# Seven-product feed-forward in all four stages, with GpSimd making the weight sums of the last one

## The chip, the cores and the metric

One core of one Trainium2 chip. The metric is the device time of one execution in microseconds (us). A program like this keeps five engines going at once: TensorE (PE; its weight loads are listed as PEld), VectorE (DVE), ScalarE (ACT), GpSimd (POOL) and SyncE (SP), which issues the DMAs. Each runs its own instructions in order and waits for the others on semaphores.

## The reference

Two transformer blocks in fp32, one after the other, at 512 latent and 256 context tokens, D = 1024. The change lies in the second block, in its feed-forward half steps:

```python
def swiglu(x, w13, w2):
    a, b = jnp.split(x @ w13, 2, axis=-1)
    return (jax.nn.silu(a) * b) @ w2

def ffn_half_step(h, g, shift, scale, gate, w13, w2):
    return h + 0.5 * gate * swiglu(modulate(rms_norm_2(h, g), shift, scale), w13, w2)

for i in range(DEPTH):                      # DEPTH = 2
    h = ffn_half_step(h, ...ffn1[i])        # latents; hc likewise for the context
    ...mixing of latents and context...
    h = ffn_half_step(h, ...ffn2[i])
    if not last:
        hc = ffn_half_step(hc, ...ffn2[i])
```

`w13` is 1024 x 5632 and `w2` 2816 x 1024. The half step runs four times: three times on all T = 768 tokens, and the last time, where the context isn't wanted any more, on 512.

## The kernel before, in words

Activations lie feature-major: 8 row tiles of 128 features x C tokens, C = 768 or 512. An fp32 product is made from three products of rounded parts: every operand is split into a high part (a rounding copy by ScalarE: `w_hi`, `x_hi`, `g_hi`) and a low part (VectorE subtracts the high one: `w_lo`, `x_lo`, `g_lo`), and `triple` issues high x high, high x low and low x high. All matmuls of these stages are 128 x 128 weights against H = C/2 columns (384 or 256), or against a full segment of up to 512.

**Units and slots.** The 2816 hidden features are 22 tiles. A unit ("g", u, 0) makes hidden tile u: its two weight tiles (a and b of swiglu) come with one DMA of 1 MB into one of two landing buffers. A unit ("w", c, j) multiplies four hidden tiles into half of the output rows, from another 1 MB. After the g units 4, 8, 12 and 16 come the two w units of the four tiles before; at the end come w units 4 and 5 (the last one only two tiles). A unit is cut into parts, and a part is a slot: 12 matmuls, with one split weight quarter of 128 x 512 in a ring (`SH`, `SL`).

**Seven products.** Plain, a unit's 2 x 2 blocks want eight quarter products. The first two g units are plain (`plain_group`, all four quarters together). The others use Strassen's form (Winograd's variant) with seven (P1 to P7), each with sums of operands: sums of the normed input (`x_sum`: three per row tile pair, and `F4`), made once a stage; sums of the weights, four a unit, which overwrite the landing buffer (`b11 = b12 - b11`, `b12 = b22 - b12`, `b11 = b22 - b11`, `b21 = b21 - b11`); and for the second product sums of the hidden tiles (`g_sum`). Weight quarter P5 can be split only when sum 1 is made, P7 after sum 2, P6 after sum 3, P4 after sum 4. The parts P4 and P3 of a unit are held back and run between the first parts of the next (`held`).

**Two functions.** `ffn_sevens` (L1388) runs the three 768-token stages, and uses seven products for the first *and* the second matmul. Its ring holds 8 slots. VectorE makes the weight sums of g units, GpSimd those of w units. `ffn` (L909) runs the last stage, 512 tokens: seven products only for the first matmul; the second is plain (L1092, eight parts a chunk of four tiles, 12 matmuls of 512 columns each), and VectorE makes the weight sums (L1257). Its ring holds 11.

**Order of the work.** Nothing plans at run time: every engine walks the same list of slots. TensorE runs `quarter`, `second` and `last_two`; ScalarE and VectorE run `after(n)`, which waits for slot n and does what is due then: copies and silus, `gated`, `add_bank`, `add_out` (a product is added to the residual, twice a slot, L1845), `g_low` (L1822), `g_sum`, and at the end `split` for the slots whose ring places are free. In a w unit a bank collects several products one after the other, and VectorE must have added the sum so far before the next product goes onto it (`out_done`). `first_done` tells that the first half of a slot is there, `slot_done` that all is.

**The opening of a stage.** ScalarE and VectorE make the normed input tile by tile, while `plain_group(0)` follows them. Then come the input sums: x_sum, ScalarE's high copy, VectorE's low part, four times in turn, and only then does either engine go on to `after(0)`, with the gates of the plain groups and the splits of slot 8 and later. `plain_group(1)` runs meanwhile.

Of the kernel before, what the change touches and what calls it, by code (L numbers as in the profile page):

```python
# [22 lines left out]
P = 128  # L23
# [367 lines left out]
class Kernel:  # L391
# [517 lines left out]
    def ffn(self, layer, which, segs, m, gain, tag, following):  # L909
# [7 lines left out]
        parts = [(c, c0, n, o, n // 2) for (c, (c0, n)), o in zip(enumerate(segs), (0, LAT // 2))]  # L917
        shift, scale, gate = m(0), m(1), m(2)
        PLAIN, RING, GR = 2, 11, 6
        A11, A21, A12, A22, S1, S2, S4 = range(7)  # L920
        S3 = A21
        P1, P2, P5, P7, P6, P4, P3 = range(7)
        operand_of = (A11, A12, S1, S3, S2, A22, S4)
        bank_of = (0, 1, 2, 0, 0, 0, 2)

        units = []
        for u in range(FT):
            units.append(("g", u))
            if u % 4 == 0 and 4 <= u <= 16:
                units.append(("w", u // 4 - 1))  # L930
        units += [("w", 4), ("w", 5)]
        slots, loads, begin = [], [], {}
        for kind, u in units:
            begin[kind, u] = len(slots)
            if kind == "g":
                loads.append((kind, u, 0))
                slots += [(kind, u, part, len(loads) - 1) for part in range(4 if u < PLAIN else 7)]
            else:
                for j in range(2 if u < 5 else 1):
                    loads.append((kind, u, j))  # L940
                    slots += [(kind, u, 4 * j + part, len(loads) - 1) for part in range(4)]
        Q = len(slots)
        last_slot = [max(q for q in range(Q) if slots[q][3] == n) for n in range(len(loads))]
        tiles_of = lambda c: range(4 * c, min(4 * c + 4, FT))
        order, held = [], []
        for kind, u in units:
            q = begin[kind, u]
            if kind == "g" and u < PLAIN:
                order += [q, q + 1, q + 2, q + 3]
            elif kind == "g":  # L950
                order += [q + P1] + held + [q + P2, q + P6, q + P5, q + P7]
                held = [q + P4, q + P3]
            else:
                order += [q] + held + list(range(q + 1, q + (8 if u < 5 else 4)))
                held = []
        assert sorted(order) == list(range(Q))
        place_of = {q: n for n, q in enumerate(order)}
        used_up = lambda q: place_of[last_slot[slots[q][3]] if slots[q][0] == "g" and slots[q][1] < PLAIN else q] + 1
        ended = lambda kind, u, part: place_of[begin[kind, u] + part] + 1
        splits_at, nxt = [], RING  # L960
        for n in range(Q):
            splits_at.append([])
            if nxt < Q and used_up(nxt - RING) <= n + 1:
                splits_at[-1].append(nxt)
                nxt += 1
            assert n + 1 == Q or order[n + 1] < nxt
        outs_before = lambda c: 8 * c

        AHt, ALt, GHt, GLt, SHt, SLt, temps, early = self.place(tag, [
            ("x_hi", 7 * 4 * 384, F32R), ("x_lo", 7 * 4 * 384, F32R), ("g_hi", GR * T, F32R), ("g_lo", GR * T, F32R),  # L970
            ("w_hi", RING * 512, F32R), ("w_lo", RING * 512, F32R), ("ffn_tiles", 3 * 384 + 2 * T, F32),
            ("x_full", 2 * GR * T, F32, 2 * 7 * 4 * 384)])
        AH, AL = (t[:, 0:28 * H].rearrange("p (o k n) -> p o k n", o=7, k=4) for t in (AHt, ALt))
        GH, GL = (t.rearrange("p (s n) -> p s n", n=T)[:, :, 0:C] for t in (GHt, GLt))
        SH, SL = (t.rearrange("p (s k n) -> p s k n", k=4, n=P) for t in (SHt, SLt))
        land = self.land
        X1, X2, X3 = (temps[:, H * n:H * n + H] for n in range(3))
        X123 = temps[:, 0:3 * H].rearrange("p (o n) -> p o n", o=3)
        SG = [temps[:, 1152 + T * n:1152 + T * n + C] for n in range(2)]
        full_at = (2, 3, 4, 5, 8, 9, 10, 11)  # L980
        F = [early[:, T * a:T * a + C] for a in full_at]
        F4 = early[:, 2 * T:6 * T].rearrange("p (k n) -> p k n", n=T)
        halves = lambda t: t.rearrange("p (h n) -> p h n", h=2)
        pair_of = lambda t, k: t[:, 2 * (k // 4):2 * (k // 4) + 2, k % 4]
        A = self.small[:, 48:64].rearrange("p (k c) -> p k c", c=2)
        half = self.small[:, 32:48].rearrange("p (k c) -> p k c", c=2)
        tt, stt, mm = nc.vector.tensor_tensor, nc.vector.scalar_tensor_tensor, nc.tensor.matmul
        bank = lambda b, n=H: PS[:, b * 512:b * 512 + n]
        spans = [(0, C)] if C <= 512 else [(0, H), (H, H)]
# [10 lines left out]
        for kind, u in units:  # L1000
            if kind == "w":
                at_bank += at_bank % 2
# [16 lines left out]
        with nc.Block() as block:  # L1019
            @block.sync  # L1020
            def _(sp):
# [7 lines left out]
                if following:  # L1029
                    sp.wait_ge(wlo.h, wlo.at(0, Q))  # L1030
# [3373 lines left out]
```

## Time and profile before

| | us |
|---|---|
| median of 3 runs (lowest, highest) | 4178.95 (4173.89, 4184.53) |
| the profiled execution: its own time | 4179.97 |
| its span | 4178.2 |
| TensorE busy | 3951.5 |
| VectorE busy | 2753.9 |
| ScalarE busy | 1827.6 |
| GpSimd busy | 373.9 |
| mean granted TensorE clock | 0.978 |

Busy is the time in which an instruction of the engine ran. Matmuls are pipelined, so that their records overlap: one of 384 columns is listed with 334 ns, though the next starts 173 ns after it. The start-to-start distance is the price. In the lists, "[0.42 <-DVE g_lo L1822]" is idle time before an instruction and who ended it.

### The profile page before, as it was taken

Reading aid. Unit: us, or ns where it says so; the run is one execution under the profiler, and the core shown is the slowest. Engines: PE = TensorE matmul, PEld = TensorE weight load, DVE = VectorE, ACT = ScalarE, POOL = GpSimd, SP = SyncE. Lnnn points to the kernel's source line nnn. Section 1 sums busy time; section 2 is a strip of 40 time slices with the busy share of each in tenths; the row PEclk is TensorE's granted clock in tenths of the full one; section 3 lists DMA queues with packets and bytes.
Section 4 is the critical chain, followed back from the end, with each engine's and each line's share of the span. In section 5 each row is a group of like instructions: output and inputs, shape, how many; then the busy total and the mean of one; then the engine's idle time right before and its main releaser. Section 6 shows DMA issues by size and latency. Waiting matters only on the chain. (4 is left out here: it accounts for less than half of the span.)

```text
span 4178.2 us, 93191 instructions
## 1 busy us (share of the span) xinstructions
PE 3951.5 (95%) x40440; PEld 3512.1 (84%) x40440; DVE 2753.9 (66%) x4362; ACT 1827.6 (44%) x3172; POOL 373.9 (9%) x279
## 2 busy tenths in 40 slices
PE   6999999998999998999999989999999999989999
PEld 5778877777788887899997768999989999668998
DVE  6555665555444443788885457888878887657776
ACT  4433433342255554544443425444454444445443
POOL 0111111011000000011111020111111111120000
PEclk9999999999999998999999999999999999999999
DMA  4001010003345455112121101221212212112222
GB/s 173 19 14 28 27 28 28 17 14 136 146 167 182 176 178 222 51 71 72 71 71 75 59 31 51 71 71 71 73 49 71 71 71 81 65 58 78 103 103 81
DMA packets 99880, 337.05 MB, mean 81 GB/s; under 512 B 5009, under 2 KB 66834, under 8 KB 71826
## 3 DMA queue, kind: packets, MB, share of 16 engines
q1 hardware_dynamic: 99474, 331.09, 22.2%
q8 instruction: 321, 5.26, 0.5%
q14 instruction: 85, 0.70, 0.1%
HBM read 326.62 MB, written 4.46 MB: 79 GB/s over the span
## 5 line engine op out<-in xcount | busy, mean ns | idle before, releaser
L1547 PE MATMUL banks<-x_hi,w_hi 128*128 128x384 f32 (+2 forms) x1968 | 662.7, 337 | 21.5 <-ACT banks L1708 7.9
L1548 PE MATMUL banks<-x_lo,w_hi 128*128 128x384 f32 (+2 forms) x1968 | 660.0, 335 | 0.0
L1549 PE MATMUL banks<-x_hi,w_lo 128*128 128x384 f32 (+2 forms) x1968 | 659.7, 335 | 0.0
L1670 ACT CAST w_hi<-landing_all 128x512 fp32r<-128x512 f32 x666 | 406.9, 619 | 463.0 <-PE banks L1549 172.9
L1787 DVE TENSOR_TENSOR w_lo<-landing_all,w_hi 128x512 fp32r<-128x512 f32 x666 | 478.8, 739 | 60.0 <-ACT w_hi L1670 58.8
L1547 PEld LDWEIGHTS banks<-x_hi,w_hi 128*128 128x128 f32 x1968 | 371.1, 189 | 31.0 <-ACT banks L1708 8.8
L1548 PEld LDWEIGHTS banks<-x_lo,w_hi 128*128 128x128 f32 x1968 | 371.2, 189 | 2.0
L1549 PEld LDWEIGHTS banks<-x_hi,w_lo 128*128 128x128 f32 x1968 | 371.1, 189 | 2.0
L1547 PE MATMUL banks<-g_hi,w_hi 128*128 128x384 f32 x840 | 283.6, 338 | 12.9 <-DVE x_res L1845 7.8
L1549 PE MATMUL banks<-g_hi,w_lo 128*128 128x384 f32 x840 | 280.9, 334 | 0.0
L1548 PE MATMUL banks<-g_lo,w_hi 128*128 128x384 f32 x840 | 280.9, 334 | 0.0
L1845 DVE SCALAR_TENSOR_TENSOR x_res<-banks,small,x_res 128x384 f32<-128x384 f32 x540 | 228.8, 473 | 12.1 <-PE banks L1549 12.1
L2193 PE MATMUL banks<-rw_x_hi_rwkv,rw_w_hi_rwkv 128*128 128x256 f32 (+1 forms) x512 | 190.7, 372 | 7.9 <-ACT small L2597 4.5
L1646 POOL TENSOR_TENSOR landing_all<-landing_all 128x512 f32<-128x512 f32 x30 | 38.8, 1293 | 1759.8 <-DVE w_lo L1787 1759.8
L1045 PE MATMUL banks<-x_hi,w_hi 128*128 128x256 f32 x624 | 179.2, 287 | 5.5 <-ACT ffn_tiles L1175 2.0
L1047 PE MATMUL banks<-x_hi,w_lo 128*128 128x256 f32 x624 | 177.2, 284 | 0.0
L2194 PE MATMUL banks<-rw_x_lo_rwkv,rw_w_hi_rwkv 128*128 128x256 f32 (+1 forms) x512 | 177.2, 346 | 0.0
L1046 PE MATMUL banks<-x_lo,w_hi 128*128 128x256 f32 x624 | 177.2, 284 | 0.0
L2195 PE MATMUL banks<-rw_x_hi_rwkv,rw_w_lo_rwkv 128*128 128x256 f32 (+1 forms) x512 | 176.7, 345 | 0.0
L1547 PEld LDWEIGHTS banks<-g_hi,w_hi 128*128 128x128 f32 x840 | 157.6, 188 | 22.3 <-issue 12.7
L1548 PEld LDWEIGHTS banks<-g_lo,w_hi 128*128 128x128 f32 x840 | 157.7, 188 | 0.0
L1549 PEld LDWEIGHTS banks<-g_hi,w_lo 128*128 128x128 f32 x840 | 157.7, 188 | 0.0
(548 smaller groups left out, 9283.5 us busy)
## 6 DMA issues: line engine op xcount, KB each, us to landing
landing_all<-in_w SPq DMA_DIRECT2D x132, 1024.0 KB, 4.8
arena_first<-in_ada_w SPq DMA_DIRECT2D x38, 2048.0 KB, 8.6
weight_ring_first<-in_rw_pair SPq DMA_DIRECT2D x32, 512.0 KB, 5.0
landing_all<-in_w_in SPq DMA_DIRECT2D x12, 1024.0 KB, 4.8
weight_ring_first<-in_da_head SPq DMA_DIRECT2D x16, 512.0 KB, 9.8
weight_ring_first<-in_da_head SPq DMA_DIRECT2D x8, 1024.0 KB, 6.2
landing_all<-in_w_out SPq DMA_DIRECT2D x8, 1024.0 KB, 4.8
x_normed_first<-in_ada_w SPq DMA_DIRECT2D x3, 2048.0 KB, 10.7
```

The costliest lines, as they stand in the source:

```text
L1045: mm(o, wh, xh, start=first, stop=False, skip_group_check=onto)
L1046: mm(o, wh, xl, start=False, stop=False, skip_group_check=onto)
L1047: return mm(o, wl, xh, start=False, stop=last, skip_group_check=onto)
L1547: mm(o, wh, xh, start=first, stop=False, skip_group_check=onto)
L1548: mm(o, wh, xl, start=False, stop=False, skip_group_check=onto)
L1549: return mm(o, wl, xh, start=False, stop=last, skip_group_check=onto)
L1670: nc.scalar.copy(SH[:, q % RING], raw(q)).then_inc(whi.h, 1)
L1787: tt(SL[:, q % RING], raw(q), SH[:, q % RING].bitcast(F32), ALU.subtract).then_inc(wlo.h, 1)
L1845: ins = stt(xs, PS[:, at + c0:at + c0 + cn], half[:, x, c:c + 1], xs, ALU.mult, ALU.add)
L2193: mm(o, wh, xh, start=kt == 0, stop=False)
L2194: mm(o, wh, xl, start=False, stop=False)
L2195: ins = mm(o, wl, xh, start=False, stop=kt == KT - 1)
```

## The change

1. `ffn` is gone, and `ffn_sevens` takes its name and a parameter `segs`; sizes follow C = 768 or 512. The last stage, at 512 tokens (H = 256), so gets seven products in the second matmul too, and the ring of 8.
2. Weight sums of g units are VectorE's only for C = 768; in the 512-token stage GpSimd makes them, as it does those of the w units.
3. The order of slots: a w unit that follows a g unit holds P3 of that unit back to behind P6, and P3 comes behind P7. In the last unit the held part comes behind the first.
4. `second` issues the two halves' first inner tile (k = 0) before it waits for the hidden tiles (`glo`), then k = 1 of both halves; so `first_done` comes after 9 of 12 matmuls instead of 6.
5. The input sums get two buffers, and are interleaved with `after(0)` to `after(4)`.
6. The banks of the last eight outputs are taken in the order in which they come free.

```diff
-    def ffn(self, layer, which, segs, m, gain, tag, following):
...
-    def ffn_sevens(self, layer, which, m, gain, tag, following):
+    def ffn(self, layer, which, segs, m, gain, tag, following):
...
+        by_vector = lambda unit: unit[0] == "g" and C == T
...
             if unit not in sevens:
-                slots += held + [(unit, part) for part in range(4)]
+                slots += [(unit, 0)] + held + [(unit, 1), (unit, 2), (unit, 3)]
...
             else:
-                slots += [(unit, P1)] + held[0:1] + [(unit, P2)] + held[1:2] + [(unit, P5), (unit, P6), (unit, P3), (unit, P7)]
+                slots += [(unit, P1)] + held[0:1] + [(unit, P2), (unit, P5), (unit, P6)] + held[1:2] + [(unit, P7), (unit, P3)] if held[1:2] else \
+                    [(unit, P1)] + held + [(unit, P2), (unit, P5), (unit, P6), (unit, P3), (unit, P7)]
...
-        first_sums = temps[:, 2 * H + 2 * T:5 * H + 2 * T].rearrange("p (o n) -> p o n", o=3)
+        first_sums = [temps[:, a:a + 3 * H].rearrange("p (o n) -> p o n", o=3) for a in (2 * H + C, 5 * H + C)]
...
     def second(q):
-                    pe.wait_ge(glo.h, glo.at(0, 4 * unit[1] + (3 if part in (P1, P2, P4) else 4)))
                     pe.wait_ge(wlo.h, wlo.at(0, q + 1))
+                    at = [bank_at(unit, part, ab) for ab in range(2)]
                     for ab in range(2):
...
-                        for k in range(2):
-                            ins = triple(bank(b), SH[:, r, 2 * ab + k], SL[:, r, 2 * ab + k], OH[:, x, k], OL[:, x, k], k == 0 and first, k == 1, not first)
+                        triple(bank(at[ab]), SH[:, r, 2 * ab], SL[:, r, 2 * ab], OH[:, x, 0], OL[:, x, 0], first, False, not first)
+                    pe.wait_ge(glo.h, glo.at(0, 4 * unit[1] + (3 if part in (P1, P2, P4) else 4)))
+                    for ab in range(2):
+                        ins = triple(bank(at[ab]), SH[:, r, 2 * ab + 1], SL[:, r, 2 * ab + 1], OH[:, x, 1], OL[:, x, 1], False, True, not first)
                         ins.then_inc((first_done if ab == 0 else slot_done).h, 1)
...
             @block.gpsimd
                 for unit, s in sevens.items():
-                    if unit[0] == "g":
+                    if by_vector(unit):
                         continue
...
                 def gate_half(u, h, src):
-                    elif u >= PLAIN:
+                    elif u >= 1:
                         act.wait_ge(sums_lo.h, sums_lo.at(0, 4))
...
             @block.scalar
-                for at in range(4):
-                    x_sums(at)
-                for n in range(Q):
+                x_sums(0)
+                after(0)
+                after(1)
+                x_sums(1)
+                after(2)
+                after(3)
+                x_sums(2)
+                x_sums(3)
+                for n in range(4, Q):
                     after(n)
...
             @block.vector
-                for at in range(4):
-                    x_sum(at)
-                    if at == 3:
-                        L.mark(tt(F4[:, :, 0:H], F4[:, :, 0:H], F4[:, :, H:T], ALU.subtract), sums_made)
-                    x_sum_low(at)
-                for n in range(Q):
+                x_sum(0)
+                x_sum(1)
+                x_sum_low(0)
+                for n in range(4):
+                    after(n)
+                x_sum(2)
+                x_sum_low(1)
+                after(4)
+                x_sum(3)
+                x_sum_low(2)
+                L.mark(tt(F4[:, :, 0:H], F4[:, :, 0:H], F4[:, :, H:C], ALU.subtract), sums_made)
+                x_sum_low(3)
+                for n in range(5, Q):
                     after(n)
```

## Rows read from the trace of the kernel before

**Rows 1.** The page, part 1: busy us (share) xinstructions by engine
```profile
PE 3951.5 (95%) x40440; PEld 3512.1 (84%) x40440; DVE 2753.9 (66%) x4362; ACT 1827.6 (44%) x3172; POOL 373.9 (9%) x279
```

**Rows 2.** Windows (stretch, length, busy by engine, PEclk, DMA): two stages, two chunks
```profile
1708.00:2215.00 507.00, 496.07 (x2814) 487.75 (x2814) 420.86 (x694) 236.57 (x414) 62.23 (x43) 0.99 0.19 69
3805.00:4170.00 365.00, 357.74 (x2442) 331.99 (x2441) 283.20 (x488) 177.02 (x354) 6.43 (x5) 0.99 0.25 90
1885.70:1974.50 88.80, 87.95 (x505) 87.28 (x505) 74.80 (x125) 40.27 (x74) 11.14 (x8) 1.00 0.20 72
3921.90:3984.40 62.50, 62.50 (x433) 58.39 (x433) 48.99 (x85) 29.32 (x60) 0.00 (x0) 1.00 0.28 102
```

**Rows 3.** Timeline of TensorE (start, duration): first and last of three unbroken runs
```profile
1829.67 0.33 PE L1548 MATMUL banks<-x_lo,w_hi 128*128 128x384 f32 x1
...
1833.84 0.33 PE L1548 MATMUL banks<-x_lo,w_hi 128*128 128x384 f32 x1
...
3899.73 0.28 PE L1045 MATMUL banks<-x_hi,w_hi 128*128 128x256 f32 x1
...
3911.13 0.28 PE L1047 MATMUL banks<-x_hi,w_lo 128*128 128x256 f32 x1
...
4151.64 0.39 PE L1045 MATMUL banks<-g_hi,w_hi 128*128 128x512 f32 x1
...
4162.29 0.39 PE L1047 MATMUL banks<-g_hi,w_lo 128*128 128x512 f32 x1
```

**Rows 4.** Waits of TensorE, 1706 to 3570 us: total, times, longest
```profile
PE banks L1547 <- ACT banks L1708: 7.9, 3, 2.6
PE banks L1547 <- DVE x_res L1845: 7.8, 15, 1.0
PE banks L1547 <- ACT ffn_tiles L1708: 7.4, 3, 3.5
PE banks L1547 <- DVE g_lo L1822: 5.1, 12, 0.4
...
PE banks L1547 <- DVE w_lo L1787: 3.5, 3, 1.2
```

**Rows 5.** TensorE around one such wait, and the window behind an opening's waits
```profile
1884.97 0.34 PE L1549 MATMUL banks<-x_hi,w_lo 128*128 128x384 f32 x1
1885.73 0.44 PE L1547 MATMUL banks<-g_hi,w_hi 128*128 128x384 f32 x1 [0.42 <-DVE g_lo L1822]
1886.01 0.34 PE L1548 MATMUL banks<-g_lo,w_hi 128*128 128x384 f32 x1
...
3101.00:3121.00 20.00, 17.54 (x90) 17.22 (x91) 18.90 (x28) 10.94 (x21) 0.00 (x0) 0.91 0.15 53
```

**Rows 6.** Timeline of VectorE in the opening of the third stage
```profile
3074.75 0.55 DVE L1854 TENSOR_TENSOR ffn_tiles<-x_full 128x384 f32<-128x384 f32 x1
...
3077.71 1.36 DVE L1861 TENSOR_TENSOR x_lo<-ffn_tiles,x_hi 128x1152 fp32r<-128x1152 f32 x1 [1.23 <-ACT x_hi L1702]
```

**Rows 7.** Timeline: VectorE beside GpSimd's weight sums, 1874 to 1894 us
```profile
1874.51 3.38 DVE L1787 TENSOR_TENSOR w_lo<-landing_all,w_hi 128x512 fp32r<-128x512 f32 x2 [0.24 <-ACT w_hi L1670]
1880.64 1.28 DVE L1787 TENSOR_TENSOR w_lo<-landing_all,w_hi 128x512 fp32r<-128x512 f32 x2
...
1892.82 1.13 DVE L1845 SCALAR_TENSOR_TENSOR x_res<-banks,small,x_res 128x384 f32<-128x384 f32 x2
...
1874.36 1.29 POOL L1646 TENSOR_TENSOR landing_all<-landing_all 128x512 f32<-128x512 f32 x1 [60.96 <-DVE w_lo L1787]
1875.73 1.62 POOL L1648 TENSOR_TENSOR landing_all<-landing_all 128x512 f32<-128x512 f32 x1
```

**Rows 8.** Groups of VectorE: one chunk of the last stage, then adds in 768-token stages
```profile
L1249 DVE TENSOR_TENSOR w_lo<-landing_all,w_hi 128x512 fp32r<-128x512 f32 x36 | 24.1, 684 | 0.4 <-ACT w_hi L1152 0.4
L1257 DVE TENSOR_TENSOR landing_all<-landing_all 128x512 f32<-128x512 f32 x17 | 11.8, 692 | 0.6
...
L1260 DVE TENSOR_TENSOR ffn_tiles<-banks,ffn_tiles 128x256 f32<-128x256 f32 x12 | 5.1, 422 | 5.5 <-PE banks L1047 3.7 <-ACT ffn_tiles L1175 1.8
...
L1845 DVE SCALAR_TENSOR_TENSOR x_res<-banks,small,x_res 128x256 f32<-128x256 f32 x120 | 56.6, 472 | 0.0
```

More of the change, by code:

```diff
@@ L916, in ffn @@
         H, rstd_at = C // 2, 6 * 512
[L917 to L960, printed above, removed]
-        for n in range(Q):
[L962 to L989, printed above, removed]
-        sig = self.sig
-        gain_ready, half_ready, own = sig("norm_gain_ready"), sig("half_gate_ready"), sig("dve_order")
@@ L1414, in ffn_sevens @@
         loads = {unit: n for n, unit in enumerate(units)}
-        sevens = {unit: unit[1] - PLAIN if unit[0] == "g" else 2 * unit[1] + unit[2] for unit in units if (unit[1] >= PLAIN if unit[0] == "g" else unit[1] < 5)}
+        by_vector = lambda unit: unit[0] == "g" and C == T
+        in_sevens = [unit for unit in units if (unit[1] >= PLAIN if unit[0] == "g" else unit[1] < 5)]
+        sevens = {unit: sum(by_vector(x) == by_vector(unit) for x in in_sevens[:n]) for n, unit in enumerate(in_sevens)}
         slots, held = [], []
@@ L1788, in split @@
                     unit, part = slots[q]
-                    if unit[0] == "w" or unit not in sevens or part not in (P1, P5, P2):
+                    if unit not in sevens or not by_vector(unit) or part not in (P1, P5, P2):
                         return
@@ L1877, in after @@
                         for x in (2 * part, 2 * part + 1)[0:1 if part == 3 else 2]:
-                            residual(x, *parts[0])
-                            residual(x, *parts[1]).then_inc(out_done.h, 1)
+                            for at in tile_parts(x):
+                                ins = residual(x, *at)
+                            ins.then_inc(out_done.h, 1)
                         if part == 3:
@@ L1956, in ffn_sevens @@
         self.advance(1, last_done)
-        self.advance(4 * (FT - PLAIN), wsum)
-        self.advance(40, wsum2)
+        self.advance(4 * sum(map(by_vector, in_sevens)), wsum)
+        self.advance(4 * sum(not by_vector(unit) for unit in in_sevens), wsum2)
         self.advance(2 * (FT - PLAIN), u_made)
```

458 lines of the change are left out of this document (47 added, 411 removed).

## The prediction, made before the changed kernel ran

> **What bounds the kernel now.** First the page, part 1: TensorE is busy in 95% of the span, VectorE in 66%, GpSimd hardly [rows 1]. Then the windows, since that is a mean over stages. In a 768-token feed-forward stage TensorE works 496 of 507 us, in the 512-token one 358 of 365; VectorE is at 83% in a 768-token chunk (74.8 of 88.8 us) and at 78% in a 512-token chunk (49.0 of 62.5) [rows 2]. So these stages run at TensorE's rate, apart from its waits. Third, TensorE's timeline, for the price of a matmul, which is its start-to-start distance: 4.17 us over 24 steps is 0.174 us at 384 columns, 11.40 over 95 is 0.120 at 256, and 10.65 over 47 is 0.227 at 512 [rows 3]. 256 columns cost more than half of 512. Fourth, its waits: in the three 768-token stages 12.9 us of idle in 27 waits of w units (15 for `x_res`, 12 for `g_lo`), and 18.8 us in nine waits of the openings, three each [rows 4]. A wait costs more than its listed idle: behind the matmul of 1884.97 the next one is due at 1885.14 and starts at 1885.73, 0.59 us late for 0.42 listed, and its successor is 0.11 late again [rows 5]. I add 0.26 us to each. Behind an opening's waits the clock row shows 0.91 over 20 us: 3.6 us at the 1.2 GHz level instead of 2.4, which costs 1.8 us of matmuls [rows 5].
>
> **Chunk order and the split in `second` (768 tokens).** At most 12.9 + 27 x 0.26 = 19.9 us come off. The `g_lo` wait is 0.6 us long, and now half a slot, 6 x 0.174 = 1.04 us, is issued ahead of it: gone. The `x_res` waits stand where P4 follows P7 of the unit before with one slot between; now there are two. The last five of them are longer (up to 1.0 us) and lie before the last unit, where a whole slot is put in between. Against it: `first_done` comes after nine matmuls, 0.52 us later, and TensorE wants the second half's bank 0.52 us sooner. VectorE's two adds take 1.1 us [rows 7] of a 2.08 us slot, so I expect room for it. The deferred P3 also frees its landing buffer two slots later, three slots or 6.2 us before the next load's first split; at 512 tokens that is 4.3 us, but the ring of 8 lies between. Bounds: 10 us (the `x_res` waits stay) to 20. I take **-18.5**.
>
> **Openings (768 tokens).** They cost 18.8 + 9 x 0.26 + 3 x 1.8 = 26.5 us. Today VectorE waits 1.23 us for ScalarE in three of the four input sums [rows 6], and neither splits slot 8 before all four are made. With two buffers the three waits go, 3.7 us an opening, and the first weights of unit 2 are early, so the `w_lo` wait (3.5 us in all) goes. What is late next: VectorE has the same work as before up to unit 3 and is behind, so it, or ScalarE, whose gates of unit 1 now wait for all four low parts, makes TensorE wait again, for the copy of P1 (about 1 us) and at P4 of unit 2 (2 to 3 us). So some 4.2 us an opening are won, of at most 8.8: **-12.5**, bounds 0 and -26.
>
> **Last stage, TensorE.** Out: 5 chunks x 96 matmuls x 0.227 = 109.0 us. In: 5 x 168 x 0.120 = 100.8. **-8** if TensorE stays the bound.
>
> **Last stage, VectorE.** A chunk becomes 42 slots of 1.44 us = 60.5 us of TensorE. VectorE's list for it: 42 splits at 0.684 (28.7), 24 adds to the residual at 0.472 (11.3), 16 sums with products and gates at 0.422 (6.8) [rows 8], and for the hidden tiles two low parts of 256 and two of 512 elements, eight sums at 0.42 and two low parts of 1024 at some 1.2: 8.0. That is 54.8 us of durations in 96 instructions. Back to back they overlap (two splits in 1.28 us, not 1.37 [rows 7]), and some wait a little for a semaphore: 48.5 us, about the 49.0 of today. Gone are 16 sums at 0.69 and eight adds at 0.75; new are six splits, 24 adds and the hidden sums. So GpSimd does not empty VectorE, it keeps it level.
>
> And GpSimd's sums, 24 a chunk, are not free for VectorE. Two splits take 1.28 us alone and 3.38 us beside sums L1646 and L1648: 1.05 us lost for a sum. Two adds that read PSUM take 1.13 us beside L1646 and lose nothing [rows 7]. So a sum costs between 0 and 1.05 us by what it meets. In g units nearly everything of VectorE's is splits and other work on SBUF: I take 0.8 for 16 sums. In w units half is adds from PSUM: 0.5 for eight. Together 16.8 us, and 48.5 + 16.8 = 65.3 > 60.5: VectorE becomes the bound. Today's chunk is 62.5, so five chunks are +14. The opening keeps its waits: unit 2's P5 and P6 now wait for GpSimd's sums of 1.29 us instead of VectorE's 0.69: +1.5. **+15.5** for the stage, bounds -9 (65.3 falls to 60.7 when the sums cost 0.5 or less each) and +40 (1.05 each in g units, 0.6 in w units: 70.1).
>
> The Trainium skill ("SBUF — State Buffer", section "Who interferes with whom") says that a VectorE instruction with two SBUF inputs and a GpSimd one that reads SBUF exclude each other for the whole instruction, whoever comes first. The trace agrees on which instructions suffer, and less on how much: a full block would make the two splits 4.0 us, and they took 3.4. By the rule the sum is that of the rival "full block".
>
> **Sum.** -18.5 - 12.5 + 15.5 = -15.5. The profiled execution took 1.8 us beyond its span of 4178.2, so 4180.0, and the median is 1.0 below: 4179 - 15.5 = 4163.5, say 4164.
>
> **Rivals.**
> *GpSimd's sums cost VectorE little* (0.5 us or less): VectorE ends a chunk in 60.5, TensorE stays the bound. For it: VectorE idles 13.5 us a chunk today, into which lost time could fall, and a third of its new work reads PSUM. Against: the splits come just when a sum is released by one. 4179 - 31 - 9 + 1.5 = 4140.
>
> *Full block*: each sum stops VectorE's SBUF work for all of its length. Sums last 1.29 to 1.62 us [rows 7]; with three quarters of them met by such work, 24 x 1.45 x 0.75 = 26 us, a chunk 74.6, +60.5 for five, in all 4179 - 31 + 62 = 4210; at 1.05 and 0.6 as above it is 4188. It decides when a sum costs over 0.84 us on average (chunk above 68.7, which eats the 31 us). For it: the 3.38 us. Against: the adds that lose nothing.
>
> *Only the place of the waits moves (768 tokens)*: VectorE at 83% is behind in openings and w units alike; the later `first_done` makes it late for P7 and P3, whose banks wait for its adds. Then 12 us come off instead of 31: 4179 - 12 + 15.5 = 4182. For it: every wait of the w units but the twelve is on VectorE's adds. Against: the distances between products of one bank grow where the waits are.
>
> **Chances.** Mine 0.47 (own range 4150 to 4178), cheap sums 0.18, full block 0.15, waits that move 0.20. From 4137 to 4192 leaves out the far end of the cheap sums and most of the full block. A difference of 0.3%, 12.5 us, is what a measurement of this kernel can tell: below 4166.5 lie six tenths of mine and nearly all of the cheap sums, 0.48 with a little of the third; above 4191.5 most of the full block and a little of the third, 0.16; between them 0.36.
>
> **What would show it.** Right: in a chunk of the last stage VectorE busy over 95% in a period of 64 to 67 us, TensorE waiting for `w_lo` or `x_res`; splits beside GpSimd's sums at 1.0 us and more; in the 768-token stages no TensorE wait for `g_lo`, hardly one for `x_res`, period 87.5; openings with one wait of 1 and one of 2 to 3 us. Wrong: a period of 60.5 (cheap sums), over 69 (full block), new waits at P7 or P3 in w units, or openings without any wait, which would be worth 14 us more than I give.

## The result and the profile after

Measured: 4244.69 us median of four runs (4237.47 to 4250.43) against 4178.95 before, a ratio of 1.016 with a 95% interval of 1.0145 to 1.0175. The change makes the kernel slower; the forecast was 4164, its range ended at 4192. It was wrong.

The page, part 1, of the kernel after (busy us, share, instructions) answers to [rows 1]:
```profile
PE 3964.6 (93%) x40800; PEld 3538.6 (83%) x40800; DVE 2827.1 (67%) x4422; ACT 1848.5 (44%) x3232; POOL 539.9 (13%) x399
```
VectorE (DVE) is 73 us busier, GpSimd (POOL) 166. A share of the span says nothing of where that hurts, so next the windows of the same stretches as [rows 2], and a chunk of a 768-token stage (stretch, length, busy by engine, PEclk, DMA):
```profile
1708.00:2215.00 507.00, 495.14 (x2832) 487.84 (x2830) 417.19 (x689) 233.76 (x412) 65.85 (x45) 1.00 0.19 69
3805.00:4170.00 365.00, 306.97 (x2367) 298.78 (x2366) 304.07 (x458) 172.20 (x349) 151.87 (x108) 0.96 0.23 81
...
1874.90:1963.90 89.00, 87.99 (x504) 87.26 (x504) 74.59 (x125) 39.69 (x73) 11.09 (x9) 1.00 0.20 72
```
The 768-token stage looks as before. In the 512-token one TensorE works 307 of 365 us instead of 358, while no other engine is full: VectorE is at 83%.

From TensorE's timeline I take each stage's length, from its first product matmul to its last. The rows for the last stage, after:
```profile
3806.06 0.47 PE L1076 MATMUL banks<-x_hi,w_hi 128*128 128x256 f32 x1
...
4233.85 0.28 PE L1078 MATMUL banks<-x_hi,w_lo 128*128 128x256 f32 x1
```
That is 427.8 us. Before it was 354.3, read the same way. The three 768-token stages were 503.7, 505.3 and 503.5 us before (1512.5 in sum) and are 503.0, 505.4 and 506.3 after (1514.7). So the last stage takes 73.5 us more and the long stages gained nothing; the rest of the spans' difference of 69.0 us (4247.2 less 4178.2) lies ahead of the first of them, which starts 6.5 us earlier in this execution, in code that the change doesn't touch.

One chunk of the last stage has two parts: the **g part**, 25 slots of gate units, and the **w part**, from the first product of its w units to the last. Windows of the second chunk, before and after:
```profile
3892.54:3930.39 37.85, 37.85 (x313) 37.53 (x312) 32.80 (x58) 21.72 (x46) 0.00 (x0) 1.00 0.31 112
3930.39:3955.08 24.69, 24.69 (x123) 20.91 (x121) 16.23 (x26) 7.60 (x14) 0.00 (x0) 1.00 0.24 86
```
```profile
3906.50:3951.92 45.42, 39.47 (x302) 38.86 (x301) 34.91 (x47) 21.91 (x48) 22.30 (x16) 0.92 0.20 71
3951.92:3982.89 30.97, 25.87 (x207) 24.80 (x205) 28.46 (x51) 12.76 (x26) 11.55 (x9) 1.00 0.29 103
```
The first pair is before: 62.5 us, TensorE always busy, VectorE at 87% and 66%. The second is after: 76.4 us, VectorE busy for 63.4 of them, but at 77% in the g part and 92% in the w part. The 42 slots of 1.44 us would be 36.0 and 24.5 us (25 and 17 slots; three of the 17 belong to gate units: the held P4 and P3, and P1 of the next one). So the g part is 9.4 us late, the w part 6.5.

Who waits, in the last stage after (waiter, releaser: us in total, times, longest):
```profile
ACT w_hi L1201 <- POOL landing_all L1182: 99.8, 29, 5.8
...
PE banks L1076 <- ACT ffn_tiles L1239: 40.7, 16, 5.1
ACT w_hi L1201 <- POOL landing_all L1177: 40.0, 26, 3.8
...
ACT w_hi L1201 <- DMA landing_all<-in_w: 38.0, 21, 3.3
...
PE banks L1076 <- DVE x_res L1382: 19.5, 22, 2.3
```
ScalarE (ACT), busy for 47% of the window of this stage shown above, stands still for 99.8 us ahead of splits (L1201) whose input is GpSimd's third sum (L1182). What queues behind it is seen at one place, on ScalarE, GpSimd and TensorE (start, duration, engine, line, output<-input, idle before and its releaser):
```profile
3867.76 0.62 ACT L1201 CAST w_hi<-landing_all 128x512 fp32r<-128x512 f32 x1 [0.53 <-POOL landing_all L1177]
3873.09 0.62 ACT L1201 CAST w_hi<-landing_all 128x512 fp32r<-128x512 f32 x1 [4.70 <-POOL landing_all L1182]
3873.61 0.37 ACT L1239 COPY ffn_tiles<-banks 128x256 f32<-128x256 f32 x1
...
3867.81 1.63 POOL L1179 TENSOR_TENSOR landing_all<-landing_all 128x512 f32<-128x512 f32 x1
3871.79 1.26 POOL L1182 TENSOR_TENSOR landing_all<-landing_all 128x512 f32<-128x512 f32 x1 [2.36 <-DVE w_lo L1324]
...
3870.08 0.28 PE L1078 MATMUL banks<-x_hi,w_lo 128*128 128x256 f32 x1
3874.03 0.58 PE L1076 MATMUL banks<-x_hi,w_hi 128*128 128x256 f32 x1 [3.68 <-ACT ffn_tiles L1239]
3874.41 0.41 PE L1077 MATMUL banks<-x_lo,w_hi 128*128 128x256 f32 x1
3874.63 0.41 PE L1078 MATMUL banks<-x_hi,w_lo 128*128 128x256 f32 x1
```
The window from there on, with the clock at the end of the row:
```profile
3874.00:3877.00 3.00, 2.97 (x14) 2.97 (x15) 2.55 (x4) 2.11 (x6) 0.46 (x1) 0.50 0.01 3
```
TensorE had ended P6 and waited for its copy (L1239) before P7. The copy stood in ScalarE's order behind the split of a P6 that is needed many slots later, which waited for GpSimd, which waited for VectorE's split of P5. TensorE is 3.8 us late for it, and its next matmuls come every 0.22 us instead of 0.12, at a granted clock of 0.50: the lower clock level (1.2 GHz), a second price of the wait. The clock of the g part of the second chunk above is 0.92, before it was 1.00.

The same happened, smaller, in the 768-token stages. After (TensorE, then ScalarE):
```profile
1874.92 0.44 PE L1076 MATMUL banks<-x_hi,w_hi 128*128 128x384 f32 x1 [0.55 <-ACT ffn_tiles L1239]
...
1904.84 0.41 PE L1076 MATMUL banks<-g_hi,w_hi 128*128 128x384 f32 x1 [0.50 <-DVE x_res L1382]
...
1873.87 0.62 ACT L1201 CAST w_hi<-landing_all 128x512 fp32r<-128x512 f32 x1 [5.03 <-POOL landing_all L1182]
1874.40 0.47 ACT L1239 COPY ffn_tiles<-banks 128x384 f32<-128x384 f32 x1
```
The `g_lo` wait of [rows 5] is gone. In its place a wait of 0.72 us for the copy stands before a gate unit's P7, and 0.67 us for `x_res` are left. From 1874.92 to the same place of the next chunk it is 89.05 us; before it was 88.74, forecast was 87.5.

### The profile page after: what moved, and what is told of

It reads as the page before. It is cut to its first block and busy times, and to the rows that moved or that the text cites. A ratio compares the mean times of both kernels' runs of the same rounds, so it can differ in the third digit from the quotient of the medians.

```text
span 4247.2 us, 94269 instructions
## 1 busy us (share of the span) xinstructions
PE 3964.6 (93%) x40800; PEld 3538.6 (83%) x40800; DVE 2827.1 (67%) x4422; ACT 1848.5 (44%) x3232; POOL 539.9 (13%) x399
## 5 line engine op out<-in xcount | busy, mean ns | idle before, releaser
L1076 PE MATMUL banks<-x_hi,w_hi 128*128 128x384 f32 (+1 forms) x2610 | 857.8, 329 | 72.7 <-ACT ffn_tiles L1239 63.9
L1077 PE MATMUL banks<-x_lo,w_hi 128*128 128x384 f32 (+1 forms) x2610 | 850.5, 326 | 0.0
L1078 PE MATMUL banks<-x_hi,w_lo 128*128 128x384 f32 (+1 forms) x2610 | 850.5, 326 | 0.0
L1201 ACT CAST w_hi<-landing_all 128x512 fp32r<-128x512 f32 x888 | 537.9, 619 | 695.9 <-POOL landing_all L1182 250.5
L1324 DVE TENSOR_TENSOR w_lo<-landing_all,w_hi 128x512 fp32r<-128x512 f32 x888 | 669.5, 772 | 128.8 <-ACT w_hi L1201 124.8
L1077 PEld LDWEIGHTS banks<-x_lo,w_hi 128*128 128x128 f32 x2610 | 501.7, 192 | 2.7
L1078 PEld LDWEIGHTS banks<-x_hi,w_lo 128*128 128x128 f32 x2610 | 501.2, 192 | 2.6
L1076 PE MATMUL banks<-g_hi,w_hi 128*128 128x384 f32 (+1 forms) x1120 | 364.5, 325 | 26.3 <-DVE x_res L1382 25.7
L1077 PE MATMUL banks<-g_lo,w_hi 128*128 128x384 f32 (+1 forms) x1120 | 360.6, 322 | 0.0
L1078 PE MATMUL banks<-g_hi,w_lo 128*128 128x384 f32 (+1 forms) x1120 | 360.4, 322 | 0.0
L1382 DVE SCALAR_TENSOR_TENSOR x_res<-banks,small,x_res 128x256 f32<-128x256 f32 (+2 forms) x660 | 278.6, 474 | 6.5 <-PE banks L1078 6.3
```

Of the source, the lines that this page charges most:

```text
L1076: mm(o, wh, xh, start=first, stop=False, skip_group_check=onto)
L1077: mm(o, wh, xl, start=False, stop=False, skip_group_check=onto)
L1078: return mm(o, wl, xh, start=False, stop=last, skip_group_check=onto)
L1201: nc.scalar.copy(SH[:, q % RING], raw(q)).then_inc(whi.h, 1)
L1324: tt(SL[:, q % RING], raw(q), SH[:, q % RING].bitcast(F32), ALU.subtract).then_inc(wlo.h, 1)
L1382: ins = stt(xs, PS[:, at + c0:at + c0 + cn], half[:, x, c:c + 1], xs, ALU.mult, ALU.add)
```

## The experiments

The theories are called A (GpSimd's results come late, and ScalarE's fixed order passes that on), B (VectorE's time beside GpSimd), C (seven products cost it in themselves). The table gives the time of the last stage's products, and of the g and w part of its second chunk with VectorE's busy time in brackets, all us, read as above. But for x14 and x15 each run is a single execution. In the eight traces with the last stage of before its length is 354.3 to 354.4 us; the long stages, and what lies ahead of them, move by a few us from one execution to the next, so I compare stages and not whole times. No kernel with the new last stage was traced twice.

| run | stage | g part | w part |
|---|---|---|---|
| before | 354.3 | 37.9 (32.8) | 24.7 (16.2) |
| after | 427.8 | 45.4 (34.9) | 31.0 (28.5) |
| x1 gate units' sums on VectorE | 417.1 | 43.6 (35.5) | 30.3 (29.0) |
| x2 all sums on VectorE | 409.9 | 40.9 (34.7) | 32.1 (29.8) |
| x3 sums of 16 columns | 359.4 | 37.1 (25.2) | 26.3 (24.4) |
| x4 the same, idle sums beside | 404.8 | 42.5 (34.1) | 29.4 (27.0) |
| x5 third landing buffer, ring 12 | 412.5 | 38.3 (32.7) | 34.2 (30.9) |
| x6 later split of P6 | 423.3 | 43.6 (34.9) | 31.6 (29.9) |
| x9 x5, splits spaced | 409.7 | 38.3 (33.6) | 33.7 (30.9) |
| x13 thinned adds | 414.9 | 46.1 (35.5) | 27.6 (24.7) |
| x16 x9 and thinned adds | 402.9 | 39.7 (32.0) | 30.2 (26.6) |
| x17 third landing buffer | 414.6 | 44.8 (32.5) | 29.8 (28.4) |
| x18 ring 12 | 448.4 | 45.9 (33.8) | 33.3 (30.1) |

**x1 and x2: who makes the sums.**
```diff
-        by_vector = lambda unit: unit[0] == "g" and C == T
+        by_vector = lambda unit: unit[0] == "g"              # x1
+        by_vector = lambda unit: unit[0] == "g" or C < T     # x2
```


> Changed from the kernel after, in the 512-token stage alone: VectorE makes the four weight sums of each of the 20 gate units again (80 sums); the 40 of the w units stay with GpSimd. Theory A (what costs is that ScalarE, in its fixed order, waits for GpSimd's sums, and copies and gates queue behind it): two thirds of those waits go; VectorE gets 16 sums of 0.69 us in a chunk and loses the overlap with as many of GpSimd's (16 x 0.62), so its own time stays near 64 us; chunk 65 to 68 us instead of 76.4, the stage's products 365 to 380 us instead of 427.8. Theory B (VectorE's time beside GpSimd, the forecast's own step): its load is unchanged within 1 us, chunk 75 to 77, stage 420 to 430. Theory C (seven products cost it in themselves at 512 tokens): no change either, 425 to 430.

> As the kernel after, but in the 512-token stage VectorE makes all 120 weight sums and GpSimd none. VectorE's list is 48.5 + 24 x 0.69 = 65.1 us a chunk without any overlap with GpSimd. Theory A and theory B both: chunk 65 to 67, VectorE over 95% busy, stage 362 to 378 us. Theory C: chunk over 72, stage over 405 us, with VectorE under 90% busy.


Measured 4236.0 and 4236.2 us (before beside them 4176.5). Stages 417.1 and 409.9: 11 and 18 us less than after, not the 50 to 65 that A and B both wanted of x2. Without any GpSimd VectorE is busy for 64.5 us of a 73.0 us chunk, 93% in the w part and 85% in the g part: theory C's case as it was put. Over x3 below, the sums cost the stage 50.5 us on VectorE and 68.4 on GpSimd. And ScalarE's stand isn't GpSimd's alone: with the sums on VectorE it waits for the third one 29 times, as in the kernel after. From x2's waits, 3842 to 4210 us:
```profile
ACT w_hi L1201 <- DVE landing_all L1337: 86.3, 29, 5.1
```

**x3 and x4: nearly no sums, and idle ones that nobody waits for.**
```diff
-                    b11, b12, b21, b22 = quarters(unit)
+                    b11, b12, b21, b22 = [b if C == T else b[:, :, 0:4] for b in quarters(unit)]
+                    # x4 alone: full subtractions between spare tiles, as many as sums, each behind its pair or single sum
```


> As the kernel after, but in the 512-token stage GpSimd's 120 weight sums cover 16 of their 512 columns each; the rest of the sums is left out. Neither their latency nor their time beside VectorE is left. Theories A and B: TensorE is the bound at about 60.5 us a chunk, stage 340 to 352 us, time 4155 to 4170. Theory C: chunk over 70, stage over 395.

> As the kernel with the 16-column sums, but after each pair or single one GpSimd runs a full subtraction of 512 columns between spare tiles that nobody reads: its 120 long operations beside VectorE are back, without anyone waiting for their results. Theory A (latency in ScalarE's order): as the 16-column kernel within 10 us, 345 to 360 us for the stage. Theory B (VectorE beside GpSimd): VectorE loses its 0.6 us per operation again and the stage is 405 to 430 us. Theory C: no difference between the two, both over 395 us.


Measured 4174.6 and 4213.4 us. With nearly free sums the stage is 359.4: so 68 of the 73.5 us hang on the 120 sums. Of these the idle operations bring back 45.4, though nobody waits for their results, so theory B has a real part. How large it is against A's, x4 can't say: its splits take 0.82 us in the mean and those of the kernel after 0.89, so the remaining 23.0 hold some of B's price too; and the short sums stand behind the idle operations in GpSimd's order, so the 45.4 hold some waiting. Of the 5.1 us left over 354.3 no run shows the cause; the short sums are still a chain, and ScalarE still stands 47.3 us for the third ones. 359.4 lies in none of the ranges expected, nearest to A's and B's (352 at most); theory C, which wanted over 395, falls. Even with nearly free sums the seven products don't give the 8 us that TensorE's matmuls save.

VectorE's groups in the last stage of the kernel after, and in x2, where GpSimd is idle (busy us, mean ns):
```profile
L1324 DVE TENSOR_TENSOR w_lo<-landing_all,w_hi 128x512 fp32r<-128x512 f32 x196 | 171.4, 894 | 43.9 <-ACT w_hi L1201 41.2
L1382 DVE SCALAR_TENSOR_TENSOR x_res<-banks,small,x_res 128x256 f32<-128x256 f32 x96 | 41.6, 472 | 0.0
L1348 DVE TENSOR_TENSOR ffn_tiles<-ffn_tiles 128x256 f32<-128x256 f32 x38 | 30.8, 849 | 0.7
```
```profile
L1324 DVE TENSOR_TENSOR w_lo<-landing_all,w_hi 128x512 fp32r<-128x512 f32 x194 | 129.3, 686 | 25.7 <-ACT w_hi L1201 24.7
L1382 DVE SCALAR_TENSOR_TENSOR x_res<-banks,small,x_res 128x256 f32<-128x256 f32 x96 | 41.8, 478 | 0.1
```
A split is 0.21 us longer in the mean in the kernel after, an add that reads PSUM not at all. 196 x 0.21 is 41 us; a gate (L1348) takes 0.85 instead of some 0.42, 38 x 0.43 = 16 us. With some 10 more in the hidden tiles' sums and low parts that is 67 us for 111 sums, 0.6 us each; forecast was 0.7. The Trainium skill ("SBUF — State Buffer", section "Who interferes with whom") says that a VectorE instruction with at most one SBUF input, outside its two-port modes, doesn't contend with GpSimd and one with two does; the trace agrees on both.

The mean of 0.21 us hides three cases. In the timelines of the two engines, 3842 to 4200 us, 128 of the 196 splits meet no sum and take 0.69 us. Sixty begin while a sum runs and take 1.35; eight begin ahead of one and take 0.68, and then it is the sum that is longer. One that begins under a sum, VectorE's row first:
```profile
3885.31 0.99 DVE L1324 TENSOR_TENSOR w_lo<-landing_all,w_hi 128x512 fp32r<-128x512 f32 x1
...
3884.13 1.62 POOL L1179 TENSOR_TENSOR landing_all<-landing_all 128x512 f32<-128x512 f32 x1
```
It ends 0.55 us behind the sum. Of the 42 that meet one sum only 37 do so too, within 0.01 us, and the other five end 0.66 us behind it. That is a full block: the split does its work when the sum has ended. The same page of the Trainium skill states it (section "SBUF: two separate sides") for the whole instruction, for a VectorE instruction with two SBUF inputs and whoever starts first; the trace agrees. A sum costs 0.6 us and not its 1.3 to 1.7 because it isn't always met: of the sums' 155 us in this window VectorE's instructions with two SBUF inputs lie beside 97, and in some of these it is the sum that waits.

**x5, x9, x17 and x18: more room between the engines.** The 512-token tiles leave room for a third landing buffer and four more slots of the ring.
```diff
-        PLAIN, RING, RAW = 2, 8, 4
+        PLAIN, RING, RAW = 2, 8 if C == T else 12, 4     # x5, x9, x18
+        NL = 2 if C == T else 3                          # landing buffers; x5, x9, x17
...
+        # x9: splits of P5 and P6 at least two slots behind the split that their sum needs
```


> As the kernel after, but the 512-token stage has a third landing buffer and a ring of 12 split weights instead of 8 (room that its smaller tiles leave free); GpSimd makes the sums as before. Theory A' (the forecast's load was right, and what it missed is that the load comes in bursts: 28.5 us of VectorE's work in the 31 us of a chunk's w part, which a ring of 8 and two landing buffers don't carry over to the g part): with more room the burst is spread over the chunk and the period falls from 76.4 towards VectorE's own 63.8 us: 66 to 70 us, stage 372 to 392 us, VectorE 92% busy or more. Rival (the waits are round trips within a unit: TensorE's product, the copy or sum of it, TensorE's next product, none of which a ring shortens): chunk 74 to 77, stage 415 to 430 us.

> As the kernel with three landing buffers and a ring of 12 in the 512-token stage, and there the splits that need GpSimd's first and third sum stand at least two slots behind the one before them in their chain, so that ScalarE doesn't stand still ahead of its copies while GpSimd works. Theory E (ScalarE's in-order stand for the chain of sums makes the waits, and depth alone only moves it forward): period falls from 72.4 to 65 to 69 us, stage 378 to 395 us instead of 412.5. Theory F (VectorE's own lateness in the w part, and its slower instructions beside GpSimd, make them): no more than 5 us from 412.5.

> As the kernel after with a third landing buffer in the 512-token stage, the ring still 8. If the g part waits because a buffer comes free late (two units' sums and the load of 4.8 us in one cycle of two buffers), it falls from 46.3 to 38 to 40 us and the chunk to 70 to 72. If ScalarE's stand for GpSimd's third sum makes it, at most 3 us go.

> As the kernel after with a ring of 12 split weights in the 512-token stage and two landing buffers. If the landing buffer's cycle makes the g part's waits, the ring gives less than 3 us a chunk (74 to 77); if the lead of 8 slots is too short for ScalarE's stands, it gives what both together gave: 71 to 73.


Measured 4225.1, 4225.1, 4227.5 and 4262.5 us (before beside them 4171.9, 4176.7, 4171.9 and 4171.9). Windows of x9, second chunk:
```profile
3905.54:3943.82 38.28, 36.36 (x303) 36.10 (x302) 33.56 (x47) 21.67 (x47) 18.95 (x14) 1.00 0.27 99
3943.82:3977.52 33.70, 27.12 (x207) 26.20 (x206) 30.88 (x51) 13.41 (x27) 15.47 (x11) 0.95 0.23 76
```
Buffers and ring together free the g part (38.3 us, 2.3 over its products) and lengthen the w part, where VectorE is busy for 30.9 us: some of its load has moved there. The period falls to 72 us and no further (x5's 412.5 us lie between the two ranges expected); the spacing gives 2.8 us of the stage and not 17 or more, so theory E of x9 falls. The landing buffer alone gives 13 us of the stage, less than expected in the g part. The ring alone, forecast harmless, costs 21 us. ScalarE's waits in x18's last stage, 3798 to 4247 us:
```profile
ACT w_hi L1206 <- POOL landing_all L1187: 75.1, 29, 5.7
ACT w_hi L1206 <- DMA landing_all<-in_w: 73.1, 21, 4.9
```
It stands less for the third sums than in the kernel after (99.8), 11 us more for the first, and 35 us more for weights that have not landed (38.0): the first split of a unit now comes earlier in its order, ahead of the landing, and copies stand behind it. TensorE waits 56 us for copies instead of 43. With a third landing buffer the same ring costs nothing: 412.5 us in x5 against 414.6 in x17. So a deeper ring behind an in-order engine is not just more slack; here the buffers that feed it had to grow with it.

**x13 and x16: VectorE's burst in the w part.**
```diff
-                    for c, c0, cn in in_half[h]:
+                    for c, c0, cn in in_half[h] if C == T else [(c, c0, 16) for c, c0, _ in in_half[h]]:
```


> As the kernel after, but in the 512-token stage the second product's adds into the residual cover 16 columns instead of 256; the rest of these adds is left out. That takes some 7 to 9 us of VectorE's time out of a chunk's w part and leaves GpSimd's sums, their latency and the queues as they are. Theory F (VectorE's burst in the w part makes the stage long): w part from 31 to 24 to 27 us, chunk from 76.4 to 66 to 70, stage 370 to 395 us. Theory E (the latency of the sums in ScalarE's order): the stage stays within 10 us of 427.8.

> The kernel with three landing buffers, a ring of 12 and the spaced splits in the 512-token stage, and there the adds into the residual thinned to 16 columns (the rest of them is left out). If the two causes add up: g part 37 to 38.3 us, w part 24 to 28 us (from 33.4), chunk 62 to 66 us against 71.6 and 73.9 with one of them alone. If VectorE's burst alone or the buffers alone were the cause and the rest a fixed chain, the chunk stays at 70 or more.


Measured 4234.3 and 4221.7 us (before beside them 4174.2 and 4171.9). A thinned add takes 0.222 us instead of 0.472, 6 us for 24 of them and not 7 to 9. The w part fell from 31.0 to 27.6, the g part stayed. The stage is 12.9 us shorter, between the two theories' numbers: F is right about the w part and says nothing of the g part. Together with the deeper buffers the period is 69.9, not the 62 to 66 of two causes that add up. So neither is the whole of it.

**x6 and x7: the split of P6 behind the copy.**
```diff
-            while nxt < Q and used_up(nxt - RING) <= n + 1 and len(splits_at[n]) < 2:
+            late = slots[nxt][0] in sevens and not by_vector(slots[nxt][0]) and slots[nxt][1] == P6
+            while nxt < Q and used_up(nxt - RING) <= n + 1 - late and len(splits_at[n]) < 2:
```
(`late` is worked out anew for each `nxt`.) x7 has the last stage as before.


> As the kernel after, but where GpSimd makes the sums the split of the sixth product's weights stands one slot later in ScalarE's and VectorE's order, behind ScalarE's copy of the g unit's sixth product. In the 768-token stages TensorE's wait of 0.72 us for that copy in each chunk and the one of 2.16 us near the end should go: each stage 3 to 5 us shorter (products 499 to 502 instead of 503.0 to 506.3). In the 512-token stage the theory of latency in ScalarE's order has up to 23 us to give (the difference between the full sums and the 16-column sums with the idle operations beside them): 405 to 422 us instead of 427.8; if VectorE's own lateness makes the waits, it stays within 5 us of 427.8.

> The 512-token stage as in the kernel before (plain second product, ring of 11, no sums by GpSimd); the 768-token stages as in the kernel after, with the later split of the sixth product. The last stage returns to 354 us of products. If the later split removes the waits for the copy, the three long stages give 3 to 5 us each and the whole is 10 to 15 us under the kernel before: 4162 to 4170 on this scale (before 4179). If the waits only move once more: 4176 to 4181.


Measured 4226.8 and 4161.5 us (before 4171.9 beside both). The three long stages take 500.4, 501.8, 499.9 and 500.0, 503.2, 501.7 us, 1502.1 and 1504.9 in sum. The kernel after's code for them ran in eleven profiled executions of this study, with sums of 1510.7 to 1516.6: it is some 11 us shorter, more than that spread, and the wait for the copy inside the chunks is gone. x7's last stage is back at 354.4. In x6's last stage only 4.5 us of the 23 between x4 and the kernel after came.

**x8 and x12: one edit of the 768-token stages undone,** the last stage as before.
```diff
+                slots += [(unit, P1)] + held[0:1] + [(unit, P2)] + held[1:2] + [(unit, P5), (unit, P6), (unit, P3), (unit, P7)]  # x8
...
+                for at in range(4):        # x12, on VectorE; on ScalarE all four x_sums(at), then every slot
+                    x_sum(at)
...
+                    x_sum_low(at)
+                for n in range(Q):
+                    after(n)
```


> The 512-token stage as in the kernel before; the 768-token stages as in the kernel after, but with the kernel before's order of the w units' products. If the new order is what puts the split of the sixth product ahead of the copy, then TensorE's 0.72 us for the copy in each chunk is gone and the waits of 0.56 to 0.59 us for x_res are back at their old places; no wait for g_lo, since the second product's halves stand apart. Stages 500 to 503 us. If the new order is worth what was forecast for it, stages 506 to 510 us.

> The 512-token stage as in the kernel before; the 768-token stages as in the kernel after, but with the kernel before's opening: all four first sums made and split before anything of the first two units is served. The forecast gave the new opening 12.5 us over three stages (4.2 each); read from the two traces, the waits of the opening were 6.4 us before and 4.3 after, and the slow clock behind the long one is in both: the new one should be worth 1.5 to 2.5 us a stage, so here 504.5 to 508.5 us of products.


Measured 4156.3 (before 4171.9) and 4192.1 (before 4176.7). Sums of the long stages: 1507.8 with the old order, so the new order costs 7 us of them instead of giving any; 1523.7 with the old opening (508.9, 509.3, 505.5), so the new opening gives 9 us, 3 a stage, more than the 1.5 to 2.5 expected. x12 also gives order and halves together: in these stages it differs from the kernel before by them and little else (the banks of the last outputs), and is 11.2 us longer. In x8 the wait for the copy is gone from the chunks and two waits for `x_res` stand there instead of one: TensorE's waits, 1694 to 3542 us,
```profile
PE banks L1555 <- DVE x_res L1861: 12.9, 27, 1.0
PE banks L1555 <- ACT ffn_tiles L1718: 10.6, 3, 3.5
```
and its chunk is 88.85 us. The `g_lo` wait is gone there too, so the halves in `second` alone remove it, and a chunk is no shorter for it than the 88.74 before.

**x10 and x11: the later split at the opening too,** the last stage as before. In the opening ScalarE stood 2.85 us for VectorE's third sum of unit 3 ahead of the copy of unit 2's P6, and TensorE 3.70 us for that copy:
```profile
1754.52 0.69 PE L1076 MATMUL banks<-x_hi,w_hi 128*128 128x384 f32 x1 [3.53 <-ACT ffn_tiles L1239]
```
```diff
+            late = slots[nxt][0] in sevens and slots[nxt][1] == P6     # x10; x11: w units and the second of the g units
```


> The 512-token stage as in the kernel before; in the 768-token stages the split of the sixth product's weights is one slot later in every unit, also where VectorE makes the sums. At the opening TensorE's wait of 3.7 us for ScalarE's copy (behind a split that waits 2.85 us for VectorE's third sum of the next unit), and the slow clock after it, should fall by 3 to 5 us a stage. Products of the stages 495 to 499 us instead of 500.0, 503.2 and 501.7; if VectorE's lateness makes that wait whatever the order, unchanged within 1 us; if the later splits run into the ring's end in the other units, longer.

> As the last one, but of the units whose sums VectorE makes only the second gets the later split. The opening's wait falls as there (3 to 5 us a stage), the steady chunks stay as they are with the later split in the w units alone: 495 to 499 us a stage.


Measured 4157.4 and 4168.3 us (before 4176.7); long stages 498.7, 499.6, 498.7 and 499.2, 500.1, 499.9. That is 3 to 8 us less in sum than x6 and x7, not 9 to 15; x14, the same kernel as x10, has 498.5, 501.0 and 501.2. TensorE in x10, first opening:
```profile
1756.05 0.44 PE L1556 MATMUL banks<-x_hi,w_hi 128*128 128x384 f32 x1
...
1763.14 0.45 PE L1556 MATMUL banks<-x_hi,w_hi 128*128 128x384 f32 x1 [2.63 <-ACT ffn_tiles L1719]
```
The wait for this copy has all but gone, and one of 2.8 us for a later copy, which it had hidden, has come.

**x14 and x15: two of these repeated.** x14 is x10's kernel, in six executions, x15 is x8's, in twelve.


> The 512-token stage as in the kernel before, the 768-token stages as in the kernel after with the later split of every sixth product. By the products of its three long stages in the first look (498.7, 499.6, 498.7 against 503.7, 505.3, 503.5) it is 15.5 us shorter than the kernel before: ratio 0.9955 to 0.9970. If the start of the stages, which moved by up to 14 us between runs for reasons outside them, made the difference of the single times, the ratio is 0.998 or more.

> The 512-token stage as in the kernel before, the 768-token stages as in the kernel after but with the kernel before's order of the w units' products. By the products of its long stages in the first look (502.0, 502.9, 502.9) it is 4.7 us shorter than the kernel before: ratio 0.998 to 0.9995. The forecast's 31 us for the three stages would be a ratio of 0.9926.


x14: 4159.88 us, ratio 0.9972 (0.996 to 0.9983), before 4174.23. x15: 4165.74 us, ratio 0.9979 (0.9967 to 0.9991). By these ratios both beat the kernel before, by 12 and 9 us, and so the kernel after; their intervals overlap. x14 gains a little less than expected (0.9970 at most), x15 a trace more (0.9980).

## Why the prediction was wrong, step by step

**"65.3 > 60.5: VectorE becomes the bound"** is the step that failed: +14 there, and +15.5 for the stage, where +73.5 came. The period is 76.4 us, with VectorE at 83% and not over 95%. Its terms were right: VectorE is busy for 63.4 us of a chunk (forecast 65.3), with nearly free sums for 49.6 (forecast 48.5), and a sum costs it 0.6 us (forecast 0.7). Wrong was to take the longest engine's load for the period. Two things that the step left out are in the rows. First, the load has phases: the w part holds 28.5 us of VectorE's work against 24.5 us of products, while the g part holds 34.9 against 36.0. Before, the heavier load lay beside the g part (32.8 of 37.9). Even with nearly free sums it is 24.4 in the w part, all that its products leave room for. More than half of it (23 adds, the hidden tiles) depends on products just ended, and a ring can't move it. x13 bears this out: with the adds thinned the w part fell by 3.4 us. Second, sums lie on a path that goes VectorE, GpSimd, VectorE, GpSimd, ScalarE in each unit, and ScalarE's copies stand behind its end. VectorE's lateness comes back as ScalarE's, and that as TensorE's and as a lower clock. "But the ring of 8 lies between" was the cover I named; x18 and x5 show that a longer one makes it worse with two landing buffers and gives 2 us with three.

**"-8" for TensorE's matmuls.** The price per matmul held (0.120 us), but even x3 doesn't get it: 359.4 us with nearly free sums against 354.3 before.

**"+1.5" for the opening of the last stage** was mis-sized: TensorE is late there by 2.2, 2.5 and 4.6 us, before by 2.1 and 2.2, so the listed waits alone are 5.0 us longer.

**"-18.5" for order and halves** failed too, and in sign: +11 by x12. The `g_lo` wait went, as said. The place given by the new order was paid at another: the w unit's P6 split now stands ahead of the gate unit's P6 copy, a queue that I had not walked through. Alone the order costs 7 us. What the halves give was not tried alone; before less the opening's 9 would be 1503.5, and x8 and x15, which add the halves, are at 1507.8 and 1506.8, so a gain is not shown.

**"-12.5" for the openings**: right in sign, 9 us in place of 12.5. The mechanism was as told (one wait of 0.65 us for P1's copy, one long one), but the long one was 3.7 us, at P7 of unit 2 and not at P4, and brought the low clock with it. The forecast's wait at P4, 2 to 3 us, lay hidden behind it: in x10 it is there, 2.8 us long. Together the three long stages gave +2.2 us instead of -31.

**The rivals.** "Only the place of the waits moves" was true of the long stages, by way of ScalarE's order and not of VectorE's adds. "Full block" was right about what happens when the two engines meet, and the prediction's reading of its own rows against it was wrong. The two splits of [rows 7] end at 1877.89, 0.54 us behind the second sum (1877.35), as a full block has it; its "4.0 us" for a full block leaves out that the second sum was held up itself (1.62 us instead of 1.29). The rival's size was not right: it had three quarters of the sums' time met, 26 us a chunk, where VectorE lost about 14. So its period of 74.6 us is near the measured 76.4 by luck: VectorE isn't full, and without GpSimd (x2) the period is still 73.0.

**Open** is how the 43.5 us between x16 (402.9) and x3 (359.4) divide. The spaced, deep and thinned kernel still has GpSimd's sums and VectorE's slower instructions; no run took the latency away and left VectorE's load and the copies' place alone. That the sums cost the stage 68 us is shown by x3; how much of it is VectorE's lost time, how much its load in the w part and how much the order of the queues is not.

## What to carry to other kernels

Compare loads by phase, as short as the buffers between the engines: here VectorE was at 83% over a chunk and had 28.5 us of work beside 24.5 us of products in two fifths of it. When a result goes to another engine for its making, look in the in-order queue of whoever consumes it for what stands behind that wait; a deeper ring alone only brought other waits forward. Before a slot order is changed, write each engine's queue around the moved slot and look for a split that passes a copy.

## What the runs showed of the hardware

A residual add of 16 columns took 0.222 us where one of 256 took 0.472. That is 1.04 ns a column, so some 0.2 us of either, nearly all of the short one, is not its columns. Two gates beside sums L1182 and L1185 took 2.72 us; gates have a mean of 0.42 each in the kernel before, so they lost 1.9 of the 2.3 us that they shared with the sums. The second ends 0.28 us behind the second sum. As with the splits that begin under a sum, the work is done when the sum has ended:
```profile
3964.48 2.72 DVE L1348 TENSOR_TENSOR ffn_tiles<-ffn_tiles 128x256 f32<-128x256 f32 x2
...
3964.19 1.29 POOL L1182 TENSOR_TENSOR landing_all<-landing_all 128x512 f32<-128x512 f32 x1 [2.01 <-DVE w_lo L1324]
3965.62 1.30 POOL L1185 TENSOR_TENSOR landing_all<-landing_all 128x512 f32<-128x512 f32 x1
```
